# Feed-forward of a two-layer diffusion backbone: the first two output tiles of a group interleaved, and the conditioning rows placed more evenly

## The reference

```python
def _conv_ffn(h, w_up, conv_w, conv_b, w_down):
    u = h @ w_up
    u = lax.conv_general_dilated(u, conv_w[:, None, :], window_strides=(1,),
                                 padding=[(CONV_W // 2, CONV_W // 2)],
                                 dimension_numbers=('NWC', 'WIO', 'NWC'),
                                 feature_group_count=u.shape[-1]) + conv_b
    a, g = jnp.split(u, 2, axis=-1)
    return (jax.nn.silu(a) * g) @ w_down
...
    for i in range(DEPTH):
        sh1, sc1, g1, sh2, sc2, g2 = jnp.split((sc @ ada_w[i] + ada_b[i])[:, None, :], 6, axis=-1)
...
        h2 = _modulate(_rmsnorm(x, norm2_w[i]), sh2, sc2)
        x = x + g2 * _conv_ffn(h2, ffn_w_up[i], ffn_conv_w[i], ffn_conv_b[i], ffn_w_down[i])
        if not last:
            ctx = ctx + cg1 * yc
            hc2 = _modulate(_rmsnorm(ctx, norm2_w[i]), csh2, csc2)
            ctx = ctx + cg2 * _conv_ffn(hc2, ffn_w_up[i], ffn_conv_w[i], ffn_conv_b[i], ffn_w_down[i])
```

## Time and profile before

| | |
|---|---|
| median of three runs | 2189.89 us |
| lowest and highest | 2188.59 and 2191.58 us |
| the profiled execution, its own time | 2191.7 us |
| its span | 2189.7 us |
| mean granted clock of TensorE | 0.966 |
| TensorE busy | 2014.5 us (92%) |
| VectorE busy | 1377.5 us (63%) |
| ScalarE busy | 763.6 us (35%) |

### The profile page before, as it was taken

The page is one execution under the profiler, slowest core; times in us unless marked ns, Lnnn a source line. Parts: engine busy times, 40 slices in busy tenths (PEclk is TensorE's granted clock), DMA queues, the critical chain, the costliest instruction groups (busy, mean ns, idle before and its releaser), DMA issues.

```text
span 2189.7 us, 30582 instructions
## 1 busy us (share of the span) xinstructions
PE 2014.5 (92%) x10688; PEld 1717.0 (78%) x10688; DVE 1377.5 (63%) x2236; ACT 763.6 (35%) x1277; POOL 96.4 (4%) x162
## 2 busy tenths in 40 slices
PE   4889999999999869999999999699999779999996
PEld 4678888887887758887888888488888658787884
DVE  5675564663664677756664556677777557557376
ACT  3423223323322334311331232365556335333232
POOL 0000000000000000000000000211011000000000
PEclk8899999999999989999999999799999889999998
DMA  6230230230231112333324314211111222222222
GB/s 266 77 106 29 91 111 17 93 113 20 78 108 36 49 48 86 96 115 130 100 96 135 106 57 136 86 50 49 53 44 34 77 67 94 88 96 96 87 96 86
DMA packets 50765, 186.40 MB, mean 85 GB/s; under 512 B 5568, under 2 KB 5568, under 8 KB 50560
## 3 DMA queue, kind: packets, MB, share of 16 engines
q1 hardware_dynamic: 37248, 136.73, 18.8%
q0 software_dynamic: 13440, 48.63, 6.8%
HBM read 181.15 MB, written 4.19 MB: 85 GB/s over the span
## 4 chain that ended last, share of the span: by engine, by line
PE 73%; DVE 12%; issue 7%; DMA 4%; ACT 3%; DVEq 0%; SPq 0%; ACTq 0%; POOLq 0%
PE acc L372 60%; PE o_ps L454 4%; PE acc L563 2%; DMA ada_raw<-in_ada_dram 2%; PE o_ps L542 2%; PE acc L443 2%; DVE pt_lo L1402 1%; DVE h_lo L1132 1%; PE o_ps L563 1%; PE acc L532 1%; DMA x<-in_x_in_dram 1%; DVE ss L1060 1%; DVE w_lo L1028 1%; DVE scratch L1123 1%; ACT w_hi L692 1%
## 5 line engine op out<-in xcount | busy, mean ns | idle before, releaser
L372 PE MATMUL acc<-h_hi,w_hi 128*128 128x512 f32 (+1 forms) x1824 | 522.0, 352 | 46.2 <-DVE h_lo L1132 38.7
L372 PE MATMUL acc<-h_hi,w_lo 128*128 128x512 f32 (+1 forms) x1824 | 516.5, 349 | 0.0
L372 PE MATMUL acc<-h_lo,w_hi 128*128 128x512 f32 (+1 forms) x1824 | 516.3, 348 | 0.0
L692 ACT ACTIVATE w_hi<-raw 128x1024 fp32r<-128x1024 f32 x232 | 244.9, 1056 | 599.0 <-PE acc L372 597.0
L1028 DVE TENSOR_TENSOR w_lo<-raw,w_hi 128x1024 fp32r<-128x1024 f32 x232 | 283.9, 1224 | 256.0 <-ACT w_hi L692 250.0
L372 PEld LDWEIGHTS acc<-h_hi,w_hi 128*128 128x128 f32 x1824 | 292.9, 189 | 103.3 <-issue 42.6
L372 PEld LDWEIGHTS acc<-h_hi,w_lo 128*128 128x128 f32 x1824 | 292.5, 189 | 46.1
L372 PEld LDWEIGHTS acc<-h_lo,w_hi 128*128 128x128 f32 x1824 | 292.3, 189 | 46.0
L372 PE MATMUL acc<-act_hi,w_hi 128*128 128x512 f32 (+1 forms) x528 | 163.2, 363 | 14.5 <-DVE act_lo L1306 12.2
L1146 DVE SCALAR_TENSOR_TENSOR x<-acc,mod,x 128x512 f32 (+3 forms) x136 | 82.0, 637 | 145.1 <-PE acc L372 140.1
L372 PE MATMUL acc<-act_lo,w_hi 128*128 128x512 f32 (+1 forms) x528 | 162.2, 361 | 0.0
(11 more groups left out here) (189 smaller groups left out, 2965.3 us busy)
## 6 DMA issues: line engine op xcount, KB each, us to landing
raw<-in_weights_dram SPq DMA_DIRECT2D x232, 512.0 KB, 3.3
ada_raw<-in_ada_dram POOLq DMA_DIRECT2D x80, 512.0 KB, 3.6
ada_start<-in_ada_first_dram SPq DMA_DIRECT2D x4, 2048.0 KB, 22.0
x<-in_x_in_dram SPq DMA_DIRECT2D x1, 3072.0 KB, 23.5
park_dram<-x POOLq DMA_DIRECT2D x1, 2048.0 KB, 8.1
rel<-in_bias_dram POOLq DMA_DIRECT2D x16, 128.0 KB, 2.4
out_dram<-x SPq DMA_DIRECT2D x8, 256.0 KB, 2.0
x<-park_dram POOLq DMA_DIRECT2D x1, 1536.0 KB, 9.6
```

Source lines behind the costliest of these rows:

```text
L372: mm = nc.tensor.matmul(tile[:, c0:c0 + cn], wt[:, b * P:(b + 1) * P], mv[:, n, c0:c0 + cn], start=(n == 0 and m == 0), stop=(n == last an ...
L692: nc.scalar.activation(w_hi[i][:, :], raw[i][:, :], ACT.Copy).then_inc(hi_split, 1)
```

## The change

The pair of output tiles that comes first in each group is taken out of the output loop on all three engines, and the loop has one trip less. On TensorE the new `outputs_start` runs it: the first tile's blocks but the last, then the second tile's first two blocks, then the first tile's last block, which is the one that waits for the up loop's last `act_lo`, then the rest of the second tile. On VectorE the first pair has its own number of conditioning rows, `FIRST_ADA`, the first of them ahead of the first `add_gated`. The rows are now 8 + 8 + 6 in the up loops, 3 + 3 + 2 in the first pairs and 2 per pair in the remaining three pairs of each group.

```diff
-UP_ADA, DOWN_ADA = (1, 1, 0), (3, 3, 2)
+UP_ADA, FIRST_ADA, DOWN_ADA = (1, 1, 1), (3, 3, 2), (2, 2, 2)
...
-                    with turns(pe, 4, A.steps(2) + [(chunk, 2)]):
-                        for m in range(2):
+                    outputs_start(size, parts, act_ready)
+                    with turns(pe, 3, A.steps(2) + [(chunk, 2)]):
+                        for _ in range(2):
                             w = next_chunk()
-                            product(open_acc(), w, range(size), act_hi, act_lo, parts, act_ready if m == 0 else None)
+                            product(open_acc(), w, range(size), act_hi, act_lo, parts)
+
+            def outputs_start(size, parts, ready):
+
+                jobs = []
+
+                def some(job, n0, n1):
+                    tile, w = jobs[job]
+                    for n in range(n0, n1):
+                        if job == 0:
+                            ready(n)
+                        for m, (wt, mv) in enumerate(((w[0], act_hi), (w[0], act_lo), (w[1], act_hi))):
+                            for c0, cn, _ in parts:
+                                mm = nc.tensor.matmul(tile[:, c0:c0 + cn], wt[:, n * P:(n + 1) * P], mv[:, n, c0:c0 + cn],
+                                                      start=(n == 0 and m == 0), stop=(n == size - 1 and m == 2))
+                    if n1 == size:
+                        mm.then_inc(acc_full, 1)
+
+                w = next_chunk()
+                jobs.append((open_acc(), w))
+                some(0, 0, size - 1)
+                w = next_chunk()
+                jobs.append((open_acc(), w))
+                some(1, 0, 2)
+                some(0, size - 1, size)
+                some(1, 2, size)
...
                     last = n == len(GROUPS) - 1
-                    pairs = 3 if ends and last else 4
+                    for m in range(2):
+                        t, after = wait_after()
+                        split()
+                        if last:
+                            final_square(t, after, 0, m, width)
+                    pairs = 2 if ends and last else 3
...
-                    loads = DOWN_ADA[n] if with_ada else 0
                     last = n == len(GROUPS) - 1
                     if last:
                         step(nc.vector.memset(ss[:, :], 0.0))
+                    loads = FIRST_ADA[n] if with_ada else 0
+                    if loads:
+                        ada_step(0, waste, conds)
+                    for m in range(2):
+                        add_gated(m, layer, 40, parts)
+                        split()
+                        if last:
+                            add_square(m, w_all)
+                        if m + 1 < loads:
+                            ada_step(m + 1, waste, conds)
+                    if loads:
+                        take_ada(1, nj, loads, conds)
+                    nj += loads
+                    loads = DOWN_ADA[n] if with_ada else 0
...
-                        if loads == 3:
-                            ada_step(2, waste, conds)
                         if loads:
                             take_ada(1, i * loads + nj, loads, conds)
```

More of the change, by code:

```diff
@@ L862, in ffn @@
                             if last:
-                                final_square(t, after, 2 * i, m, width)
-                    if pairs == 3:
+                                final_square(t, after, 2 * i + 2, m, width)
+                    if pairs == 2:
                         for m in range(2):
@@ L1311, in ffn @@
                     own_done()
-                    pairs = 3 if ends and n == 2 else 4
-                    loads = DOWN_ADA[n] if with_ada else 0
+                    pairs = 2 if ends and n == 2 else 3
                     last = n == len(GROUPS) - 1
@@ L1320, in ffn @@
                         for m in range(2):
-                            add_gated(2 * i + m, layer, 40, parts)
+                            add_gated(2 * i + 2 + m, layer, 40, parts)
                             split()
@@ L1326, in ffn @@
                                 ada_step(m, waste, conds)
-                        if loads == 3:
-                            ada_step(2, waste, conds)
                         if loads:
                             take_ada(1, i * loads + nj, loads, conds)
-                    nj += 4 * loads
-                    if pairs == 3:
+                    nj += 3 * loads
+                    if pairs == 2:
                         for m in range(2):
```

## The result

The changed kernel takes 2161.23 us, the median of four runs (2160.4 to 2162.91); the kernel before took 2190.73 us beside it (2188.59 to 2191.69). The ratio is 0.9868, with a 95% interval of 0.9853 to 0.9883: faster by 29.5 us, where 23 us were forecast. The time lies 0.8 us under the low end of the range. The profiled execution has a span of 2158.4 us, against 2189.7 us.

The account below looks back on a forecast made before the run. TensorE carries 73% of the span, so time is gained where it waits or runs slowly in the feed-forward stages. 8.3 + 6.75 + 7.5 = 22.6 us, 23 with vanished waits' overlap, gives 2167 us; range 2162 to 2173.

Parts of the forecast that it names:

- Step 1: At the six feed-forward borders, two second-tile blocks ahead of the first tile's last block shrink TensorE's act_lo waits: 8.3 us.
- Step 2: In the output loop of layer 0's first group, re-placed conditioning rows remove all three TensorE waits for w_lo: 6.75 us.
- Step 3: In the feed-forward stages, shorter waits remove four TensorE stretches at the lower clock: 7.5 us; only the last border's fall remains.
- The four slow stretches: Lower-clock TensorE stretches behind the 3.35 and 3.07 us waits and the 1.88 us wait and its twin: 7.5 us.
- the fifth: Clock fall behind the last border, layer 1's group of 6, forecast to stay behind a 1.9 us wait: 1.6 us.
- Step 4: ScalarE only has its first pair written out ahead of the loop, its splits having the same waits: costed at nothing.
- Step 5: TensorE's list grows by 396 matmul rows and their weight loads; code fetches cost 0, bounds 0 and 4 us.
- the last fall: Clock fall behind the 1.9 us wait at the last border, forecast to remain; its absence gives 1.6 us more.
- a rival that makes the change slower: TensorE stalls for code at twelve feed-forward loop crossings, 36 us come back: 2203 us; chance 0.03.
- The wait that is replaced: Third tile's weights come late behind VectorE's step: 2172 us if both groups of 6 lose, 2183 if all six; chance 0.08.
- the loads stopped binding: Rival: conditioning rows' loads still bind, so w_lo waits and their clock fall stay: 2175 us; chance 0.06.
- the clock fell behind none of the remaining waits: Rival: the clock falls behind the small remaining waits too, or at shifted phases: 2171.6 us; chance 0.05, within the forecast's share.

## Why the prediction was right and wrong

**Step 1, TensorE's order: right.** Four idle rows of 1.00, 0.48, 0.48 and 1.87 us were left of six, each within 0.03 us of the forecast. (The step says that it leaves out the 0.16 us for each wait that vanishes; the sum has 0.8 us for them.) The reasoning that a wait shrinks by exactly the work put in front of it holds as long as the next wait has cover.

**Step 2, the conditioning rows: right.** All three waits for w_lo are gone, and the run with the interleaving alone brings 4.66 us of them back. That is less than the 6.75 us of the kernel before. It may be that the first pair's first row, now reduced before the first tile is full, lets the run of loads start sooner, but this isn't shown: with the rows of the kernel before in their old places, and memsets added, these waits made 5.71 us (44) and 5.36 us (128), so they differ by over 1 us without it. The risk named there, weights of the third tile behind VectorE's step, did not come about at two blocks. At three it did, at the two places and nearly with the sizes that the cover gave.

**Step 3, the clock: right in kind, wrong in one term.** The four slow stretches of 7.5 us went. I held that the fifth stays, because both waits of 1.88 us had one. It went in all four profiles that have this border with 1.87 or 1.88 us (the changed kernel twice, the interleaving alone, and the one with 84 instructions more): 1.6 us more gained. Two of two such waits had a fall in the kernel before and with 128 instructions more, one of two in the kernel with the rows alone, none of two with 44 instructions more. So the length of such a wait doesn't decide whether it has a fall, and two cases were too few to take it as a rule. That its place in time decides is a guess that no run here isolates. This was the bound that the text had worked out, and the range's low end had it in. One more fall went that the text had not listed: at the norm behind layer 0 the matmul that sums the squares took 2.93 us (x4) at half clock in the kernel before and 1.56 us (x4) at full clock in the changed one, 1.4 us in all.

**Step 4, ScalarE: right.** No idle row of TensorE at a border or in an output loop of the changed kernel names ScalarE.

**Step 5, code: the step that failed.** It looked at TensorE's code alone, and only for a cost, with bounds of 0 and 4 us. The runs show a gain, on VectorE, in a stage that I had declared untouched: "the only places that the change touches" was true of the work and not of the code's place. In the changed kernel the gain is 3.1 us, at the two returns of the attention loop. Moving the kernel before by 44 instructions takes the same stalls away (3.2 us in its profile; 4.8 us by the ratio, with clock falls in it); moving it by 128 leaves them and brings nothing; moving the changed kernel on to 128 brings them back, doubled. The rows were in the trace of the kernel before, as idle rows of VectorE without a releaser at a loop's return, and I had listed TensorE's idle rows only inside the feed-forward stages. The forecast with this term, without the last fall and without the fall at the norm is 2167 - 3.1 - 1.6 - 1.4 = 2160.9 us, against 2161.23 us. Only the last fall was within the bounds; the code's 3.1 us is the largest term of the miss.

The rule of the Trainium skill (Runtime: NRT & Kernel Launch, Instruction fetch mechanics) on taken branches out of the blocks at hand was weighed as a rival that makes the change slower, at TensorE's twelve loop ends. There nothing came of it. The traces agree with the rule at another place, the return of VectorE's attention loop, and with the other sign: 1.28 and 1.25 us there in the kernel before, with packets of code fetched at each return, and no stall and no packet in the changed one.

**The rivals.** None of them came. The wait that is replaced needs a third block; the loads stopped binding though the longest landing of a row was still 7.8 us; the clock fell behind none of the remaining waits; TensorE has no idle row without a releaser in the feed-forward stages. What both parts are worth: the interleaving 0.0105 and the rows 0.0056 of the time of before, each with the code's shift of 0.0022 in it. Counted once, that makes 0.0139, against 0.0132 measured for both, so the two parts do not need or hinder each other within the intervals. The 0.0022 is the run with 44 instructions more, clock falls included.

## What to carry to other kernels

A wait at the border of two stages is filled with work from the next output, and the amount that pays can be read beforehand: it ends where the following wait (here the weights of the third tile) has no cover left. Before forecasting an edit, list the idle rows without a releaser at the returns of all loops that lie behind the edit in program order, on every engine, since longer code ahead moves them all. And a difference of under 0.5% between two kernels is first to be checked against a kernel with instructions added that do nothing.

## What was not expected of the hardware

- Code placement: 44 idle memsets of 0.06 us each took two stalls of 1.28 and 1.25 us away at the returns of a later loop, and made a kernel of 2189 us faster by 4.8 us (3.1 to 6.8). The stalls stay with a shift of 128 instructions. With them VectorE's code is fetched in each pass of the loop, 11 or 12 packets in 190 us; without them it isn't fetched at all there.
- A clock fall is not a property of the wait alone: 1.87 us had one in 5 of 12 cases over the eight profiles in which such a wait occurs, 3.28 us in 3 of 4. No wait of up to 1.18 us at a border had one.
- TensorE's pace in a loop of the same matmuls at full clock has two values. Seventy microseconds in the first and the second up loop of layer 0 (columns as in the earlier trace rows), in the kernel before:

```profile
850.00:920.00 70.00, 70.00 (x406) 61.15 (x405) 52.67 (x73) 27.30 (x42) 2.12 (x4) 1.00 0.32 103
1050.00:1120.00 70.00, 70.00 (x398) 60.74 (x397) 45.43 (x64) 22.86 (x39) 2.12 (x4) 1.00 0.27 90
```

and in the changed kernel:

```profile
850.00:920.00 70.00, 70.00 (x398) 60.74 (x397) 51.44 (x71) 28.02 (x43) 2.12 (x4) 1.00 0.28 96
1050.00:1120.00 70.00, 70.00 (x405) 61.73 (x404) 46.70 (x63) 23.80 (x40) 2.12 (x4) 1.00 0.30 97
```

That is 406 or 398 matmuls, 1.04 or 1.06 us for a block, and it holds for a whole loop. In the second profile of the changed kernel the first loop has 405. The same program shows both, so it isn't the order; a slow loop costs some 2 us, and this may be part of the 3 us or more by which runs of one kernel differ. What sets it stays open.
